# Two chunks interleaved by pairs of weight blocks, two memory pieces turned by transfers, constants issued by GpSimd

## What is computed

```python
def rmsnorm(x, g):
    xf = x.astype(jnp.float32)
    y = xf * lax.rsqrt(jnp.mean(xf * xf, axis=-1, keepdims=True) + EPS)
    return (y * g.astype(jnp.float32)).astype(x.dtype)

def memory_cross_attention(q, mem_n, w_kv):
    kv = mem_n @ w_kv
    k, v = jnp.split(kv, 2, axis=-1)
    ...
h = rmsnorm(x, g_mix_pre[l])
proj = h @ w_in[l]
...
y_cross = memory_cross_attention(xq, rmsnorm(mem, g_mem[l]), w_mem_kv[l]) @ w_cross_out[l]
```

## Time and profile before

| | us |
|---|---|
| median of 3 runs (1643.9 to 1644.34) | 1643.91 |
| the profiled execution's own time | 1644.2 |
| its span | 1642.4 |
| PE busy in the span | 1632.2 |
| DVE, ACT, POOL busy | 1012.9, 831.2, 54.7 |

### The profile page before, as it was taken

One profiled execution on the slowest core, in us unless ns is written; L12 is line 12 of the kernel. 1 busy time (PEld: TensorE's weight loads), 2 busy tenths in 40 slices (PEclk: granted clock), 3 DMA queues, 4 the chain that ended last, 5 costly groups with the idle time before them and its releaser, 6 DMA issues.

```text
span 1642.4 us, 22325 instructions
## 1 busy us (share of the span) xinstructions
PE 1632.2 (99%) x7285; PEld 1348.8 (82%) x7285; DVE 1012.9 (62%) x1366; ACT 831.2 (51%) x1052; POOL 54.7 (3%) x117
## 2 busy tenths in 40 slices
PE   9999999999999999999999999999999999999998
PEld 7888888888888888888888888888888888888886
DVE  5664565655566576665655757677676677644544
ACT  6744444444444444444444655666656665543442
POOL 2500000000000000000000000000000000000000
PEclk9999999999999999999999999999999999999999
DMA  8877766777665765666666477777777776655653
GB/s 275 283 220 208 204 182 190 227 213 222 190 205 192 238 221 187 209 227 217 218 203 216 149 218 216 212 216 220 220 215 217 217 227 214 236 192 169 214 197 136
DMA packets 207017, 346.19 MB, mean 211 GB/s; under 512 B 28697, under 2 KB 51562, under 8 KB 206442
## 3 DMA queue, kind: packets, MB, share of 16 engines
q1 hardware_dynamic: 200265, 341.96, 66.5%
q0 software_dynamic: 2048, 2.10, 0.4%
q10 hardware_dynamic: 4640, 1.33, 0.3%
HBM read 318.02 MB, written 2.10 MB: 195 GB/s over the span
## 4 chain that ended last, share of the span: by engine, by line
PE 99%; DMA 0%; DVE 0%; issue 0%; POOL 0%; DVEq 0%; ACT 0%; SPq 0%; ACTq 0%; POOLq 0%
PE PS L1450 29%; PE PS L1452 29%; PE PS L1451 28%; PE PS L1575 3%; PE PS L1573 3%; PE PS L1574 3%; PE PS L1611 1%; PE PS L1609 1%; PE PS L1610 1%; PE PS L1527 0%; PE PS L1516 0%; DMA raw<-in_w_mem_kv_dram 0%; PE PS L1679 0%; PE PS L1678 0%; PE PS L1680 0%; PE PS L1595 0%
## 5 line engine op out<-in xcount | busy, mean ns | idle before, releaser
L962 DVE TENSOR_TENSOR w_lo<-raw,w_hi 128x1024 fp32r<-128x1024 f32 x567 | 690.3, 1224 | 569.7 <-ACT w_hi L592 568.2
L592 ACT ACTIVATE w_hi<-raw 128x1024 fp32r<-128x1024 f32 x567 | 597.2, 1059 | 630.8 <-PE PS L1452 562.7
L1450 PE MATMUL PS<-w_hi,hT_hi 128*128 128x512 f32 x1504 | 587.6, 391 | 0.0
L1452 PE MATMUL PS<-w_hi,hT_lo 128*128 128x512 f32 x1504 | 585.2, 389 | 0.0
L1451 PE MATMUL PS<-w_lo,hT_hi 128*128 128x512 f32 x1504 | 585.1, 389 | 0.0
L1450 PEld LDWEIGHTS PS<-w_hi,hT_hi 128*128 128x128 f32 x1504 | 282.3, 188 | 60.9 <-issue 2.7
L1452 PEld LDWEIGHTS PS<-w_hi,hT_lo 128*128 128x128 f32 x1504 | 282.3, 188 | 58.9
L1451 PEld LDWEIGHTS PS<-w_lo,hT_hi 128*128 128x128 f32 x1504 | 282.3, 188 | 58.4
L1450 PE MATMUL PS<-w_hi,act_hi 128*128 128x512 f32 x336 | 130.9, 390 | 0.0
L1452 PE MATMUL PS<-w_hi,act_lo 128*128 128x512 f32 x336 | 130.7, 389 | 0.0
L1451 PE MATMUL PS<-w_lo,act_hi 128*128 128x512 f32 x336 | 130.7, 389 | 0.0
(11 more groups left out here) (217 smaller groups left out, 1290.6 us busy)
## 6 DMA issues: line engine op xcount, KB each, us to landing
raw<-in_w_up_dram SPq DMA_DIRECT2D x176, 512.0 KB, 4.0
raw<-in_w_in_dram SPq DMA_DIRECT2D x112, 512.0 KB, 4.1
raw<-in_w_gate_dram SPq DMA_DIRECT2D x96, 512.0 KB, 4.5
raw<-in_w_down_dram SPq DMA_DIRECT2D x88, 512.0 KB, 4.1
raw<-in_w_mem_kv_dram SPq DMA_DIRECT2D x32, 512.0 KB, 5.8
raw<-in_w_o_dram SPq DMA_DIRECT2D x32, 512.0 KB, 3.7
up_moved<-up_stage SPq DMA_DIRECT2D x352, 32.0 KB, 2.7
raw<-in_w_conv_out_dram SPq DMA_DIRECT2D x16, 512.0 KB, 3.7
```

The costliest lines, as they stand in the source:

```text
L592: nc.scalar.activation(w_hi[i % RING][:], raw[i % RING][:], ACT.Copy).then_inc(hi_ready, inc)
L962: nc.vector.tensor_tensor(w_lo[i % RING][:], raw[i % RING][:], w_hi[i % RING][:].bitcast(F32), ALU.subtract).then_inc(lo_ready, inc)
L1450: nc.tensor.matmul(o, a_hi, b_hi, start=first, stop=False)
L1452: last = nc.tensor.matmul(o, a_lo, b_hi, start=False, stop=last_k)
```

## The change

1. The blocks of chunks 0 and 1 are interleaved in pairs (`PAIRED`): blocks 0 and 1 of chunk 0, blocks 0 and 1 of chunk 1, blocks 2 and 3 of chunk 0, and so on. Both use the same activations, so piece p of the memory is first needed at block 4p and not at block 2p. Chunk 0 ends with block 13, and ACT reads it out at block 16 (before at block 11).
2. PE turns only piece 1 (behind block 1). Pieces 2 and 3 take the way of x: copied by ACT at blocks 3 and 5, moved by POOL, turned by DVE at blocks 8 and 11, and split at once, `hi` and `lo` at blocks 8 and 11 too.
3. x's pieces follow in the same two staging tiles: copied at 10, 14, 18, 22, turned at 17, 21, 25, 29, `hi` one block later, `lo` two.
4. The nine constants are issued by POOL, first in its program, as soon as block 0's `lo` is written. DVE's work on them goes from block 8 to block 10.
5. On SP the loads of memory pieces 2 and 3 go behind weight blocks 3 and 4. The row sums of squares of `mem` on ACT are at blocks 6 and 10 (before 6 and 7).

```diff
-    X_COPY = [8, 13, 18, 23]
+    PAIRED = [(c, KB * p + r) for p in range(NCH) for c in range(2) for r in range(KB)]
+    PIECES = [("mem", 2), ("mem", 3)] + [("x", g) for g in range(NCH)]
+    COPY_AT = [3, 5, 10, 14, 18, 22]
+    TURN_AT = [8, 11, 17, 21, 25, 29]
+    HI_AT = [8, 11, 18, 22, 26, 30]
+    LO_AT = [8, 11, 19, 23, 27, 31]
...
+        def chunk_block(c, i):
+            return PAIRED[c * CB + i] if c < 2 else (c, i)
...
-                    elif c == 0 and i < NCH:
-                        mem_columns(i * CW, (i + 1) * CW, mem_in[i])
+                    elif c == 0 and i in (1, 3, 4):
+                        g = (1, 3, 4).index(i) + 1
+                        mem_columns(g * CW, (g + 1) * CW, mem_in[g])
...
-                    if c == 0 and i == NCH + 1:
-                        constants()
...
+            def constants():
+                pool.wait_ge(lo_ready, 1)
+                for dst, src in (...):
+                    pool.dma_start(dst, src).then_inc(vec_in, 16)
+                pool.dma_start(up_rows[0:2 * FK, :, :], ...).then_inc(up_rows_in, 16)
+                for n, l in enumerate((lambda_q1, lambda_k1, lambda_q2, lambda_k2)):
+                    pool.dma_start(lam_rows[:, n, :], l[0].partition_broadcast(P)).then_inc(lam_in, 16)
...
+            def move_piece(e):
+                pool.wait_ge(x_copied, e + 1)
+                if e >= 2:
+                    pool.wait_ge(prep_turned, 2 + e - 1)
+                for a in range(P // SQ):
+                    for m in range(P // SQ):
+                        pool.dma_start(x_moved[e % 2][...], x_stage[e % 2][...]).then_inc(x_moved_in[e % 2], 16)
+
+            constants()
+            move_piece(0)
+            move_piece(1)
             pool.wait_ge(squares, 2)
             rms(r_mem[:], sq_mem[:], D)
-            for g in range(NCH):
-                move_x(g)
+            for e in range(2, len(PIECES)):
+                move_piece(e)
...
-                    if i == 3 and c:
+                    if c == 2 and i == 0:
+                        after_projection(0)
+                    if i == 3 and c >= 2:
                         after_projection(c - 1)
...
-                    if c == 0 or c == NCH:
-                        pe.wait_ge(prep_lo, (0 if c == 0 else 2 * NCH) + i + 1)
-                    multiply(c * CB, i, CB, ..., lambda t: acc[:, t, :])
+                    cc, kb = chunk_block(c, i)
+                    acc = ACC[cc % 2]
+                    if c < 2 or c == NCH:
+                        pe.wait_ge(prep_lo, (0 if c < 2 else 2 * NCH) + kb + 1)
+                    multiply(c * CB, i, CB, ..., lambda t: acc[:, t, :], kb=kb)
...
-                    if c == 0 and i in (0, 1, 3):
-                        turn_memory((0, 1, 3).index(i) + 1)
+                    if c == 0 and i == 1:
+                        turn_memory(1)
```

More of the change, by code:

```diff
@@ L686, in _ @@
                         for t in range(NT):
-                            last = nc.scalar.activation(x_stage[g % 2][:, :, :, t, :],
-                                                        x_sb[:, t, g * CW:(g + 1) * CW].rearrange("p (b m n) -> p m b n", b=BPC, n=SQ), ACT.Copy)
+                            last = nc.scalar.activation(x_stage[e % 2][:, :, :, t, :],
+                                                        (mem_sb if what == "mem" else x_sb)[:, t, g * CW:(g + 1) * CW].rearrange("p (b m n) -> p m b n", b=BPC, n=SQ), ACT.Copy)
```

97 lines of the change are left out of this document (44 added, 53 removed).

## The result

The changed kernel takes 1649.5 us (median of 8 runs, 1648.8 to 1650.0) where the kernel before takes 1644.1 in the same job: ratio 1.0032, 95% interval 1.0024 to 1.0041. The forecast was 1643.5 and its range ended at 1646.5: wrong in size and in sign. The profiled execution took 1649.86 us with a span of 1648.1, 5.7 us more than the earlier trace rows.

A forecast was written before the change was run, and what follows sets the result against it. PE was taken to bound the kernel, busy 1632.2 of 1642.4 us. Turns -1.76, block 8 0 and block 12 +1.3 gave -0.4 against the profiled execution, set against the median 1643.91: 1643.5 us, range 1642.3 to 1646.5.

The forecast's parts named there:

- The end: Behind PE's last work: the prediction had no term there, so no cost was counted.
- The two turns, -1.76: Early blocks on PE: two of three turns removed at 0.88 us each, 1.76 us gained.
- POOL's constants, 7 us between 4.5 and 14: POOL from 8.4 us: issuing nine constants takes 7 us, bounds 4.5 and 14, leaving POOL free at 15.4.
- Rival (b): POOL pays by rows: constants 14 us, block 8 waits 6.4, block 12 another 1.5; 1650.0 us; chance 0.11.
- Block 5: No wait was priced there; the working checked block 4's `lo`, 19.6 against 21.1, then block 8.
- Piece 2: landing 29.1, block 8 waits 0: At block 8: piece lands at 29.1, operands ready 3.3 us later at 32.4, PE wants them at 32.6.
- Rival (d): Piece 2 lands after 7.5 us, not 5.5; block 8 waits 1.8; 1645.4 us; chance 0.17, shared with constants of 8 to 11.
- DVE's own position: Before piece 2's turn: `lo` of block 8 bounds the chain only if the piece lands before 28.4.
- Block 12, 1.3 us: A 15.8 us chain over ACT and DVE readies block 12's `lo` at 44.9; PE wants it at 43.6.
- the turn of piece 3 at 39.7: On DVE before block 12: piece 3 lands by 37.0, before DVE reaches its turn, adding nothing.
- The rest, 0: Chunk 0's reading-out, squares, DVE's constants and x's last piece cost nothing, with cover of 3 us or more each.
- wait anywhere behind block 16: A sign named beforehand: a PE wait showing behind block 16 would make the prediction wrong.

The follow-up runs named there:

- e10: The changed kernel with memory pieces 2 and 3 turned by PE again, behind blocks 4 and 6; 1645.00 us, ratio 1.0005.
- e1: The kernel before with 41 more one-row transfers issued by POOL behind `r_x`, output unchanged; 1647.69 us, ratio 1.0021.
- e4: The kernel before with only the nine constants issued by POOL once block 0's low part is written; 1644.77 us, ratio 1.0003.
- e7: The changed kernel with the second sum of squares of `mem` on ACT at block 12 instead of 10; 1647.65 us, ratio 1.0021.
- e3: The changed kernel with the nine constants issued by SP again, behind block 5's load; 1648.56 us, ratio 1.0030.
- e9: The changed kernel with constants on SP behind load 7, pieces 2 and 3 turned at blocks 7 and 9, second squares at block 12; 1649.85 us.
- e11: The changed kernel with constants on SP behind block 5's load, second squares at block 12, x's loads two blocks later; 1647.16 us, ratio 1.0020.
- e12: The changed kernel with only memory piece 3 moved, piece 2 turned by PE behind block 4, second squares at block 12; 1646.03 us, ratio 1.0013.
- e15: e14 with the first sum of squares on ACT at block 9 instead of block 6; 1646.33 us, ratio 1.0015.
- e5: The changed kernel with each piece moved by 4 transfers of 128 rows instead of 16 of 32; 1650.69 us, ratio 1.0041.
- e6: The kernel before with x's pieces moved by 4 transfers of 128 rows each instead of 16 of 32; 1643.80 us, ratio 0.9998.
- e14: e12 with 4 transfers of 128 rows a piece and the constants on SP behind block 5's load; 1644.89 us, ratio 1.0005.

## Why the prediction was wrong, step by step

Three terms were put too low. The end was put at nothing and cost 3.4 us. The weights' loads were taken to land as before; they landed late, and this made the waits at blocks 5 and 8, put at 0, which cost 0.86 and 0.97 (5 to 8 in the table). And the stretch behind block 12, put at 0, cost 1.1.

**The two turns, -1.76.** Right: 0 to 4 is 1.73 us shorter, and e10, which puts them back, returns to 90.51.

**The end: the step that failed most.** The sum knew only terms on PE and put nothing at the end, since no operation of the change lies there. POOL's drain took 3.4 of the 5.4 us (e1: 3.5 by itself). What could have been seen: between the landing of the last result and the end of the span of the kernel before lie 0.8 us that no row explains, and the change raises POOL's transfers from 64 to 105.

**POOL's constants, 7 us between 4.5 and 14.** They took 5.3: the lower bound was nearer, rows count for little (0.74 us for the first, then 0.50 to 0.58 for 1 to 128 rows, 0.85 for 264). POOL had to wait for ACT's copy anyway, so the constants did not delay the move. The sentence of the Trainium skill (DMA: Bandwidth & Descriptors, Anatomy of one DMA) that generating descriptors costs little before many are emitted agrees with these rows. Rival (b) falls. Only the issue was priced, though, and not what the packets do to the load beside them.

**Block 5 was not in the sum at all.** The working checked block 4's `lo` and then went to block 8. But block 5's load is issued as soon as its buffer is free, at 11.5, and lands 10.7 us later, not 7.2. The wait is 0.86 us, about the cover which the removed turn had given (e4 and e10 have the same late load and no wait). That the two sizes agree is chance: where that load took 12.0 us (e7), block 5 waited 1.7. It is a gain that was given back before it was had.

**Piece 2: landing 29.1, block 8 waits 0.** The transfers were forecast well. POOL's move went at 15.57, forecast 15.8; the last landing came 5.6 us after its issue, forecast 5.5; the piece was there at 28.5, 0.6 us early. Rival (d), a later landing of the piece, did not happen in this kernel (in e3, e9 and e11 the last move took 6.4 to 7.3 us). From the turn on, `memT_hi` and `memT_lo` take the 3.3 us worked out (30.94 to 34.27). The term that failed is DVE's own position, put at 28.4 and so out of play: DVE, busy with `w_lo` of block 8, could turn only at 30.94, 2.5 us later. The chain that led to 28.4 took the weights to be there when ACT wants them. They were not: ACT's heap behind raw block 5 (10.7 us from issue to landing, before 7.2) lasted until 28.1, and raw block 8 (9.2 us, before 4.6) landed at 28.7. With raw block 5 in time (e3), raw block 8 alone holds the turn until 30.47. Against the forecast landing the turn is 1.8 us late. Block 8 waited only 0.64 of that because block 5 had already waited: with that gone, e3 has 1.32 and e11 1.56.

**Block 12, 1.3 us.** Right in place, releaser and size: 1.11 us idle for `w_lo`, 1.32 by the table. That it fits so closely is in part chance, as for a block 8 that had to wait the prediction's own figure is 1.5. The forecast chain named the sum of squares between the two turns, and e7 takes it out and the wait with it. The chain itself took 15.6 us from the turn of piece 2 to block 12 (30.94 to 46.58), forecast 15.8. On the way the prediction has DVE reach the turn of piece 3 at 39.7; its own terms give 39.3, which changes nothing, as that piece had landed (37.6) when DVE was there (41.06).

**The rest, 0.** This step failed too: it cost 1.1 us, at block 19 and in small pieces to block 32: the "wait anywhere behind block 16" that the prediction named as a sign against it. The wait ahead of block 12 makes the next loads late, and ACT later waits for raw blocks. This chain is argued, but e7 bears it out by its absence, 91.72 for 0 to 32 with no wait behind block 8.

**What stays open.** In 17 kernels no stretch of 0 to 32 was shorter than 90.51, though with one turn less PE's work is 89.64 and with two 88.76. The waits always came to as much as the turns removed, or more. The runs show for each which operand was late, that raw blocks 8 to 11 land 2 to 4 us later where piece 2 is moved (e10 against the changed kernel), and that the DMA engines are mostly fuller from 20 to 40 us where a memory piece is moved (0.86 to 1.04) than where none is (0.78 to 0.87). That full DMA engines are the cause, and not for example the second queue beside SP's, was not shown by itself: e11 took 512 KB out of the stretch and block 8 waited as long, and a smaller move of a memory piece that leaves them room was not run. Moving only piece 3 (e12 to e15) still met a wait. Nor is it settled why 4 large moves make the weights' loads later than 16 small ones (e5), when in the kernel before they do not (e6).

No version beat the kernel before by more than its uncertainty. The nearest is e6, 1643.80, and it has the small spread as well; of e14 only single executions were as short (1643.5), its median was not.

## What to carry to other kernels

Account for the end of the kernel when work goes to another engine's queue: POOL has a closing price for each transfer that it issued, however long ago, and it is free only as far as another engine ends later; SP had none to be seen. A turn or other small work on the bounding engine is also cover for whatever arrives just behind it; before taking it away, look at each of the next operands and by how much it is early, not only at the one the change touches. Price a move also by what it does to the landings of the loads beside it, however idle the issuing engine is: here two moves of 512 KB, in a stretch whose DMA engines had a fifth of room, came with landings of raw blocks 2 to 4 us later. And of two operands that meet at one block, check the one that you do not move as well.

## What the runs showed of the hardware

- POOL's closing drain grows by 0.082 us for each transfer that POOL issued, from 1.38 us at 16 to 8.65 at 105, whether the transfer has one row or 128, and over 1400 us after it was issued. SP's lasts 0.01 us behind over 1300 transfers.
- A DMA issue by POOL took 0.50 to 0.58 us for 1 to 128 rows and 0.85 for 264.
- Nine small transfers on POOL's queue made a 512 KB load on SP's land after 10.5 to 12.0 us (seven kernels); with the same nine on SP's own queue behind that load it landed after 7.0 to 7.6 (ten kernels).
- DVE's turn of a piece written with a step of four took 1.99 us, contiguous 1.42.
- After 3.2 us without work, PE's granted clock fell to 0.50 for 3.4 us (e9, 36.8 to 40.2), which cost 1.6 us.
